# Two fused transformer blocks in fp32: order of turned-probability copies, memory halves and exponentials in the attention steps

## What is computed

```python
# block 1, per layer: window attention with sinks (SWA) and top-k attention (DSA), 8 heads each
s = jnp.where(mask, q @ k.T * D**-0.5, NEG); m = jnp.maximum(s.max(-1), sink)
pr = jnp.exp(s - m); o = (pr / (pr.sum(-1) + jnp.exp(sink - m))) @ v
# block 2, per layer: MLA attention, selected (SLC) and window (WIN) attention, compressed keys (CMP),
# then cross attention to a memory whose keys and values are
k, v = jnp.split(memn @ wkv, 2, axis=-1)
```

## Time and profile before

| | before |
|---|---|
| median of 3 runs | 1551.29 us (1550.52 to 1552.45) |
| profiled execution, time | 1550.02 us |
| its span | 1548.2 us |
| mean granted TensorE clock | 0.997 |
| TensorE busy | 1484.7 us, 96% of the span |
| VectorE, ScalarE, GpSimd busy | 69%, 50%, 8% |
| DMA | 265.03 MB, 171 GB/s |

### The profile page before, as it was taken

One profiled execution on the slowest core, in us unless ns is written; L12 is line 12 of the kernel. 1 busy time (PEld: TensorE's weight loads), 2 busy tenths in 40 slices (PEclk: granted clock), 3 DMA queues, 4 the chain that ended last, 5 costly groups with the idle time before them and its releaser, 6 DMA issues.

```text
span 1548.2 us, 21682 instructions
## 1 busy us (share of the span) xinstructions
PE 1484.7 (96%) x8433; PEld 1257.4 (81%) x8433; DVE 1062.9 (69%) x1713; ACT 777.0 (50%) x1162; POOL 123.1 (8%) x98
## 2 busy tenths in 40 slices
PE   8989999999899999999999999999999999999997
PEld 5767888888677888877878988888788789888886
DVE  7777588667866787676355566878863455677777
ACT  4563544444554444433665344666545653456563
POOL 0130000000310000011032000000010320000000
PEclk9999999999999999999999999999999999999999
DMA  7524655656335655644625734556536157345551
GB/s 259 198 99 139 218 190 190 213 167 203 106 120 180 228 190 191 230 155 135 191 63 165 245 131 167 191 190 218 180 116 190 47 167 250 132 168 183 189 189 65
DMA packets 184429, 265.03 MB, mean 171 GB/s; under 512 B 7368, under 2 KB 139398, under 8 KB 184200
## 3 DMA queue, kind: packets, MB, share of 16 engines
q1 hardware_dynamic: 178712, 258.38, 50.2%
q10 hardware_dynamic: 5616, 5.26, 1.0%
HBM read 258.38 MB, written 5.24 MB: 170 GB/s over the span
## 4 chain that ended last, share of the span: by engine, by line
PE 74%; DVE 14%; ACT 4%; issue 3%; DVEq 3%; POOL 1%; ACTq 0%; POOLq 0%; DMA 0%; SPq 0%
PE psw L815 18%; PE psw L814 8%; PE psw L742 7%; PE psw L744 7%; PE psw L743 7%; DVE wlo L1740 5%; PE psa L742 4%; PE psa L744 4%; PE psa L743 4%; PE psa L876 3%; PE psa L874 2%; POOL rstd L2395 1%; DVE sy L1826 1%; PE psa L929 1%; PE psw L818 1%
## 5 line engine op out<-in xcount | busy, mean ns | idle before, releaser
L1740 DVE TENSOR_TENSOR wlo<-raw,whi 128x2048 fp32r<-128x2048 f32 (+3 forms) x199 | 449.6, 2265 | 125.5 <-ACT whi L1352 125.0
L815 PE MATMUL psw<-xboth,whi 128*128 128x512 f32 x1344 | 465.0, 396 | 1.9 <-DVE wlo L1740 1.9
L1352 ACT ACTIVATE whi<-raw 128x2048 fp32r<-128x2048 f32 (+3 forms) x199 | 375.0, 1885 | 178.4 <-PE psw L744 90.5
L814 PE MATMUL psw<-xboth,wlo 128*128 128x256 f32 x1176 | 328.1, 279 | 0.0
L815 PEld LDWEIGHTS psw<-xboth,whi 128*128 128x128 f32 x1344 | 242.8, 188 | 50.3 <-DVE wlo L1740 3.4
L814 PEld LDWEIGHTS psw<-xboth,wlo 128*128 128x128 f32 x1176 | 221.7, 189 | 7.5
L742 PE MATMUL psw<-whi,xboth 128*128 128x512 f32 (+3 forms) x472 | 182.7, 387 | 6.9 <-DVE wlo L1740 5.3
L744 PE MATMUL psw<-whi,xboth 128*128 128x512 f32 (+3 forms) x472 | 179.3, 380 | 0.0
L743 PE MATMUL psw<-wlo,xboth 128*128 128x512 f32 (+3 forms) x472 | 179.3, 380 | 0.0
L1414 ACT ACTIVATE r<-psw 128x512 f32<-128x512 f32 x88 | 52.2, 594 | 173.2 <-PE psw L815 164.2
L742 PE MATMUL psa<-whi,rr 128*128 128x512 f32 x352 | 137.7, 391 | 1.4 <-DVE rr L2370 1.4
(11 more groups left out here) (290 smaller groups left out, 2183.2 us busy)
## 6 DMA issues: line engine op xcount, KB each, us to landing
raw<-in_w_gu SPq DMA_DIRECT2D x44, 1024.0 KB, 5.1
raw<-in_ffn_w_up SPq DMA_DIRECT2D x42, 1024.0 KB, 5.1
raw<-in_w_down SPq DMA_DIRECT2D x22, 1024.0 KB, 4.9
raw<-in_ffn_w_down SPq DMA_DIRECT2D x22, 1024.0 KB, 4.9
raw<-in_w_in SPq DMA_DIRECT2D x20, 1024.0 KB, 5.3
raw<-in_xa_wkv SPq DMA_DIRECT2D x16, 1024.0 KB, 5.4
raw<-in_w_o SPq DMA_DIRECT2D x8, 1024.0 KB, 5.1
raw<-in_w_out SPq DMA_DIRECT2D x8, 1024.0 KB, 5.3
```

The lines of the kernel that those rows point to most:

```text
L814: pe.matmul(bank[:, 0:S], wl[:, k, cols], xhi[:, k, :], start=False, stop=False)
L815: ins = pe.matmul(bank.rearrange("p (i s) -> p i s", i=2), wh[:, k, cols], xboth[:, :, k, :], start=k == 0, stop=k == KD - 1)
L1352: nc.scalar.activation(tile_flat("hi", i), tile_flat("raw", i), ACT.Copy).then_inc(hi_ready, 1)
L1740: v.tensor_tensor(tile_flat("lo", i), tile_flat("raw", i), tile_flat("hi", i).bitcast(F32), ALU.subtract).then_inc(lo_ready, 1)
```

## The change

TensorE makes a memory half ahead of the turns: in an odd step right behind the scores, in an even step behind the value products. ScalarE does the filler, the copies of the turned probabilities and the copy of the memory half ahead of the exponentials of the step; only the DMA of the half is issued behind them. Three steps of the `whi` and `wlo` splits move.

```diff
-HI_STEPS = {1: (7, 8, 9), 2: (10, 11, 13)}
-LO_STEPS = {1: (8, 9, 10), 2: (12, 13, 14)}
+HI_STEPS = {1: (6, 8, 9), 2: (10, 12, 13)}
+LO_STEPS = {1: (7, 9, 10), 2: (11, 13, 14)}
...
-                    half_ahead = block == 2 and i - first == SLOTS2[0]
-                    if not half_ahead:
-                        filler(i - first)
                     half_now = memory_slot(block, l, i - first)
-                    if half_ahead:
+                    if half_now is not None and i % 2:
+                        if block == 2 and i - first == CMP_STEPS[2] + 1:
+                            filler(i - first)
                         half_in_step(half_now)
+                    if block == 1 or i - first != CMP_STEPS[2] + 1:
                         filler(i - first)
...
+                    if half_now is not None and i % 2 == 0:
+                        half_in_step(half_now)
                     if first <= i - 2 < first + count:
...
-                    if not half_ahead and half_now is not None:
-                        half_in_step(half_now)
...
+                    filler(i - first)
+                    if first <= i - 2 < first + count:
+                        n = i - 2
+                        for m in range(chunk0[n], chunk0[n + 1]):
+                            act.wait_ge(pt_done, m + 1)
...
+                            nc.scalar.activation(pt[:, m % 4, :], psa[:, m % 2, :], ACT.Copy).then_inc(pt_ready, 1)
+                    half = memory_slot(block, l, i - first)
+                    if half is not None:
+                        memory_store(half, stage[block - 1][:, half % 2, :], send=False)
                     if i < first + count:
...
-                    filler(i - first)
-                    if first <= i - 2 < first + count:
...
                     if half is not None:
-                        memory_store(half, stage[block - 1][:, half % 2, :])
+                        memory_send(half, stage[block - 1][:, half % 2, :])
```

More of the change, by code:

```diff
@@ L1418, in p_out, with memory_store @@
                 nc.scalar.activation(pT[l], bank2(psw, bank), ACT.Copy).then_inc(p_ready, 1)
-            def memory_store(n, place, src=psa[:, 3, 0:TC]):
+            def memory_store(n, place, src=psa[:, 3, 0:TC], send=True):
                 if n % 2:
@@ L1428, in memory_store, with memory_send @@
                 nc.scalar.activation(place, src, ACT.Copy).then_inc(kv_staged, 1)
+                if send:
+                    memory_send(n, place)
+            def memory_send(n, place):
                 act.wait_ge(kv_staged, n + 1)
@@ L1443, in attention @@
                                                  ACT.Copy).then_inc(mix_hi, 1)
+                    filler(i - first)
[3 more added lines that the diff above has]
+                            act.wait_ge(pt_done, m + 1)
+                            if m >= 4:
+                                owner = max(x for x in range(len(chunk0) - 1) if chunk0[x] <= m - 4)
+                                act.wait_ge(pv_done, owner + 1)
+                            nc.scalar.activation(pt[:, m % 4, :], psa[:, m % 2, :], ACT.Copy).then_inc(pt_ready, 1)
+                    half = memory_slot(block, l, i - first)
+                    if half is not None:
+                        memory_store(half, stage[block - 1][:, half % 2, :], send=False)
                     if i < first + count:
```

## The result

The changed kernel takes 1534.85 us (median of 4 runs, 1534.65 to 1535.21) against 1550.91 us before (4 runs, 1550.52 to 1552.45): ratio 0.9895, 95% interval 0.9878 to 0.9912. The forecast started from 1551.29 us for the kernel before; counted from the 1550.91 measured beside it, the gain is 16.06 us, where the range ended at 16. In the profiled executions it is 1534.85 against 1550.02 us, 15.2 us.

A forecast was written before the change was run, and what follows sets the result against it. The prediction took TensorE, busy 96% of the span, as the bound, with its waits at the turns to win. Two block 1 stages at 1.5 us and two block 2 stages at 2.5 gave 8.0: 1551.3 to 1543.3 us, range 1535.3 to 1551.

The forecast's parts named there:

- What bounds the kernel: TensorE, busy 96% of the span; its waits at the turns, about 21 us of gaps in four stages, can be won.
- TensorE, next in line with the value products, waits 2.1 us: Block 1, step 7: the turns' copy stands behind the moved `whi` split until 107.6, a new TensorE wait of 2.1 us.
- the value products, which nothing hides now, wait 0.75: End of block 1's stage: the last value products wait 0.75 us for the last turn's second copy.
- Block 2's gaps: Block 2 stages: old waits of 4.2 us replaced by new ones of 1.7, a gain of 2.5 us per stage.
- 4.2: TensorE's old waits in a block 2 stage: 0.89, 1.61, 1.38 and 0.34 us, all expected to go.
- the 0.2 and 0.7: New block 2 waits for copies: value products of steps 6 and 12, 0.2 us; the last value products, 0.7 us.
- VectorE's floor in block 1: VectorE's scores and top-k search set the pace to the last maximum; the turn near 90.7 newly waits 1.6 us.
- Exponentials behind half, turn and copies are covered: Odd steps: probabilities ready 10.3 us behind their scores, needed after 13.2, about 3 us spare where step i + 2 has a half.
- the slow rival: Late exponentials hold VectorE 1.85 us in steps 3, 5 and 7 of block 1: 1554.4 us, or 1559; chance 0.08.
- Moved splits at nothing: The `whi` and `wlo` splits' new steps, with the DMAs, put at nothing; a late split costs at most 1.9 us.
- The split meets the multiplication: Rival: the split starts first, making each stage's last turns 2.0 us later, less 1.0 cover: 4 us, 1547.3; chance 0.09.
- The sum and its range: Gains of 1.5 us per block 1 stage and 2.5 per block 2 stage: 8.0 us; range 1535.3 to 1551.

The follow-up runs named there:

- experiment 1: The changed kernel, but the value products of a pair of steps wait for the copies of both steps ahead of the first; 1540.14 us.
- Experiment 4: The kernel before with ScalarE's new order alone, TensorE's order as before, so the half stays behind the turns; 1562.57 us.
- experiment 2: The changed kernel with the `whi` and `wlo` splits back in their old steps; 1534.90 us.
- Experiment 6: The changed kernel with the first `whi` split of block 1 in step 4 instead of step 6; 1540.09 us.
- experiment 5: The changed kernel, but ScalarE copies the memory half behind the exponentials again; the turn copies stay ahead; 1550.35 us.
- experiment 9: Changed kernel with block 1's first `whi` split in step 4, half copied ahead of turn copies, plus VectorE's reciprocal ahead of the maximum in steps 2 to 6; 1545.75 us.
- experiment 7: The changed kernel with block 1's first `whi` split in step 4 and its `wlo` split in step 8 instead of 7; 1533.17 us.

## Why the prediction was wrong, point by point

The direction, the mechanism and most of the places were right; the size was half. The steps:

- *What bounds the kernel.* Right. TensorE's waits at the turns were the store to draw on, nearly all passed to the end: 13.35 us in the stages, 15.1 in the span.
- *"TensorE, next in line with the value products, waits 2.1 us"* and *"the value products, which nothing hides now, wait 0.75"* (and 0.7 in block 2). **This is the step that failed.** The value products of a pair were taken as one wait for both steps' copies. The code waits per step, and the first step's products, 0.66 us for 4 heads of a t0 unit and about 1.0 of a t1 unit, run while the second copies are made. Measured: 1.17 us and nothing. The kernel with the forecast's wait gives back 5.3 us (4.4 by the stages) and has its 1.86 and 0.83.
- *Block 2's gaps.* The term "4.2" left out the gap of 0.17 us; with it the waits before are 4.4. Of the forecast new waits (1.7) the filler measured 0.32 for 0.4, the turn of step 7 0.33 for 0.4, and the 0.2 and 0.7 are absent. The stage without a fall of the clock gained 4.15 us instead of 2.5; with the pair's wait put back (experiment 1) it gains 3.3. The other 0.8 us are the gap left out (0.2), new waits of 1.24 us (0.32, 0.18 and 0.74) where 1.7 were forecast, and 0.27 us less of TensorE's busy time in the stage (56.90 against 57.17).
- *VectorE's floor in block 1.* Right, to 0.02 us for the turn at 90.7, and shown by leaving the search out. The wait itself was sized wrong: 1.6 us forecast, 2.35 to 2.49 where the clock held, since TensorE came there earlier than worked out, and 0.83 in the first profile, where a fall had slowed it. As VectorE sets the time of that turn, nothing behind it changed by this.
- *Exponentials behind half, turn and copies are covered.* Right; no wait of VectorE for them grew into TensorE. Experiment 4 shows the price without the cover, 12 us slower. At 1562.57 us it lies above what was given for the slow rival (1554 to 1559), and it came by another path: the turns waited for the multiplications, and most of the time went into falls of the clock, which the prediction has nowhere.
- *Moved splits at nothing.* Right for the time (experiment 2); by the stages they bring 0.3 to 0.4 us in each, 1.3 in all.
- *The split meets the multiplication.* Right that it wouldn't here; the distance was 0.44 us (109.02 to 109.46) where 0.9 was worked out. Experiment 6 makes it happen at another multiplication: it costs 5.2 us. That the rival's 4 us is near this is luck. They were four stages at 1.0 us of waiting; it was two stages, 2.3 us of waiting more and the falls behind it.
- *The sum and its range.* 8.0 us forecast. The pair's wait adds 4.4. The sizes in block 2 add 1.7 over two stages, less 1.6 for the clock there, block 1 about 0.8, which I can't divide further, and 1.8 lie outside the stages, mostly the clock in the profile of before: 8.0 + 4.4 + 0.1 + 0.8 + 1.8 = 15.1. The lower end of the range kept the 0.7 at the end of block 2 as certain; that was the same misreading, and without it the range would have begun at 1533.9 and held the result.

## What to carry to other kernels

When a filler that needs nothing is put ahead of a waiting operation, ask what the filler itself blocks: here it needs its one bank emptied, and the gain stands or falls with that 0.4 us copy (experiment 5: all of it). When waits are counted, read for each semaphore which value each instruction waits for, not the group it stands in. And when work is moved earlier on one engine, look at what it releases on another: a split made two steps earlier let VectorE's subtraction start 0.17 us ahead of GpSimd's multiplication and cost 5 us, more than half of it through TensorE's clock, and one constant more took that back and, by the medians, 1.6 us besides. The same meeting, the other way round, spoiled experiment 9.

## What the runs showed of the hardware that I had not expected

TensorE's granted clock fell from 2.4 to 1.2 GHz for 3.4 us at places that differ between executions of one kernel, while its time stays within 0.2%. Many falls stand during or behind waits of 1.1 us and more, but no length of a wait decides it here: the third of the kernel after (760.5 us) stands behind two waits of 0.60 and 0.61 us, one of experiment 6 (774.4 us) has TensorE busy without a wait over 0.15 us for 8 us ahead of it, and in the kernel before no fall follows the waits of 2.40 and 1.86 us in block 1. A fall ahead of a wait for VectorE is nearly free (the wait of that turn shrinks from 2.49 to 0.73 us in experiment 7, and the stages differ by 0.16). A kernel's stages must be compared with the clock of each window beside them, since one fall, 1.6 us, is as large as many a gain in this study.

A VectorE operation on 4 columns that takes 0.17 us took 1.03 us when it began beside a running GpSimd multiplication (experiment 9). It doesn't show as a wait of VectorE in the profile, since the operation itself is longer; only its length against that of its like tells.
